# Expert rows put into block order during the mixer, and experts from the third on loading plain blocks, in a one-layer hybrid encoder step

## The chip, the cores and the metric

The kernel runs on one core of one Trainium2 chip. The metric is device time in microseconds (us) of one execution, the median of several. Times inside an execution are microseconds from the first instruction of the profile.

## The reference

One encoder layer runs over 1,104 tokens of width 1024: 64 sample tokens with a carried state, and a prompt of 16 meta and 1024 ordinary tokens. Everything is float32.

```python
xn = rmsnorm(x, norm_mix)
mix = token_mixer(xn, ...)        # trailing pooling + gated linear attention, then w_out
h = x + mix
hn = rmsnorm(h, norm_ffn)
# hier_moe: one expert group of 4, then the top 2 of its 8 experts, with gates
g = argmax(softmax(hn @ w_rg + b_rg)); top_i = top_k(le of group g, 2)
for each expert e of 32:          # D = 1024, hidden width 512
    y = (silu(xb @ w_eg[e]) * (xb @ w_eu[e])) @ w_ed[e]     # xb: the rows routed to e
h = h + sum of the two experts' rows, each times its gate
y = rmsnorm(h, norm_final)
```

Each expert takes about 69 rows on average (two picks of 1,104 tokens over 32 experts).

## The kernel before

Tokens lie in 9 tiles of 128 rows (48 rows of the first are padding). The kernel has two long stages, a passage between them and an end.

**The mixer** (`body(i)` on every engine, 0 to about 475 us) handles a tile in 51.5 us. TensorE (PE) projects, VectorE (DVE) does gates, recurrences and routing, ScalarE (ACT) the activations, GpSimd (POOL) the window sums (`windows`, L472 to L483). The tail of tile j runs inside the body of later tiles: ACT's `back_h(j)` writes the normalised rows into the tile `hs` (L642) and stores them twice (once for each pick) into the DRAM tensor `hn_rows` (L646); `back_route` finds the experts; in `body(j + 2)` DVE's `back_rank(j)` gives each row its rank in its expert's list, PE's `mark` turns ranks into a table `idx_f` (row numbers of each of 96 slots of each of 32 experts), and `back_idx` adds it up.

**The passage** (about 475 to 492 us). The last tile is finished piecewise: `own_added`, `own_turned` and `router_own` for its router, `back_route` (L946 to L973), then `ranks(8)` on PE (L1443), `last_rank` on DVE (L1005 to L1015), `mark(8)` on PE (L1449), and `idx_i` (L1097) with the final indices. POOL waits for `idx_i` and gathers the rows of expert 0 and 1 by indirect DMA (L502), PE turns expert 0's rows (`turn_rows`, L1260), DVE scales them (`rows_turned`, L1113), and the first `up` starts (L1564). PE runs idle matmuls in the gaps (`keep_busy`).

**The experts** (about 492 to 1033 us). For each of 32 experts PE does the gate product (128 matmuls), the up product (128), the turning of the next expert's rows, and the down product. Buffers alternate by `b`. The hidden values come over ACT and DVE: ACT takes exp of the gate product (L735), DVE forms the silu (L1120 to L1122) and multiplies the two halves of the up product (L1126), which `down` waits for (`hid_ready`). POOL gathers the rows of an expert when a buffer is free, and scatters an expert's results to `pick_rows` (L513). SP, whose program is in order, issues the three weight loads of each expert (2 MB each): gate (L410) when the gate product two experts back is done, up (L416) when its up product is done, down (L419) when its down product is done. The passage's own order on SP is: gate, up and down of expert 0 and gate of expert 1 from 440.7 us; then it waits for `pe_half_out` and expert 0's rows before up and down of expert 1.

**The end** (about 1033 to 1082 us): each tile's two result rows are loaded, combined, normalised and stored.

Buffers are shared between the stages: `ye[0]`, into which ACT writes the results of even experts, is the tile `kz_v`; `ye[1]` is `hs`; `rows[0]` is `window_work`; `rows[1]` is `xs`.

Of the kernel before, what the change touches and what calls it, by code (L numbers as in the profile page):

```python
# [28 lines left out]
P = 128  # L29
# [35 lines left out]
PICK_ROWS = PICKS * TILES * P  # L65
OUT_ROWS = [SAMPLE] + [P] * (TILES - 1)
# [6 lines left out]
START_BUSY, ROUTE_BUSY, GATHER_BUSY = 54, 24, 34  # L73
# [12 lines left out]
           ("valid", 1), ("block_edge", EXTRA_PER_E), ("iota_x", EXTRA), ("edge_x", EXTRA)]  # L86
# [8 lines left out]
def constants():  # L95
# [16 lines left out]
    put("pick", p + TILES * P * np.arange(PICKS)[None, :] - NO_ROW)  # L112
    put("valid", (p < SAMPLE) | (p >= SAMPLE + PADS))
    put("block_edge", BLOCK * (1 + np.arange(EXTRA_PER_E))[None, :])
# [43 lines left out]
def build(nc, x_all, state_pool, state_gla, norm_mix, w_in, w_gate_up, b_gate, w_pool, pool_scale, gla_norm, w_out,  # L158
          norm_ffn, w_router, b_router, w_eg, w_eu, w_ed, norm_final, const,
          y_prompt, y_sample, pool_prompt, gla_prompt, pool_sample, gla_sample):  # L160
    hn_dram = nc.dram_tensor("hn_rows", (PICK_ROWS, D), F32, kind="Internal").ap()
    y_dram = nc.dram_tensor("pick_rows", (PICK_ROWS, D), F32, kind="Internal").ap()

    with ExitStack() as ctx:
# [131 lines left out]
        rowsT = [xnT[:, :, 0:BLOCK], hnT[:, :, 0:BLOCK]]  # L296
        sig = mixT[:, 0:3, :].rearrange("p k n -> p (k n)")
# [5 lines left out]
        rows_idx = [sb(f"rows_idx{b}", [BLOCK, 1], I32) for b in range(2)]  # L303
# [8 lines left out]
        def lot(n):  # L312
# [9 lines left out]
            pe_router pe_rank pe_idx pe_half_out pe_own_T pe_first_rows pe_hist_T pe_small_T  # L322
# [6 lines left out]
            pe_eT pe_g pe_u2 pe_d sig_ready hid_ready eT_ready ye_ready row_idx_ready  # L329
# [9 lines left out]
        out_ready = [sem(f"out_ready{i}") for i in range(TILES)]  # L339
# [14 lines left out]
        def _(sp):  # L354
# [46 lines left out]

            sp.wait_ge(s["s_sample_ready"], 1)
# [5 lines left out]
            def load_weights(t, b):  # L408
                e = 2 * t + b
                sp.dma_start(wg[b], w_eg[bass.ds(e * D, D), :].rearrange("(p k) n -> p k n", k=KD)).then_inc(g_in[b], 16)  # L410
                if isinstance(t, int) and b == 1:
                    sp.wait_ge(s["pe_half_out"], 2)
                    sp.wait_ge(rows_in[0], 16)
                if not isinstance(t, int):
                    sp.wait_ge(s["pe_u2"], 2 * (e - 1))
                sp.dma_start(wu[b], w_eu[bass.ds(e * D, D), :].rearrange("(p k) n -> p k n", k=KD)).then_inc(u_in[b], 16)  # L416
                if not isinstance(t, int):
                    sp.wait_ge(s["pe_d"], e - 1)
                sp.dma_start(wd[b], w_ed[bass.ds(e * FF, FF), :].rearrange("(k p) n -> p k n", p=P)).then_inc(d_in[b], 16)  # L419

            sp.wait_ge(s["pe_v"], TILES)
            load_weights(0, 0)
            load_weights(0, 1)
# [6 lines left out]
            with sp.Fori(1, NE // 2) as t:  # L430
                for b in range(2):

                    sp.wait_ge(s["pe_g"], 2 * t + b - 1)
                    load_weights(t, b)
# [17 lines left out]
            for i in range(TILES):  # L452
                for k, y in ((0, y1[i]), (1, y2[i])):
                    at_row = (k * TILES + i) * P
                    sp.dma_start(y[0:OUT_ROWS[i], :], y_dram[at_row:at_row + OUT_ROWS[i], :]).then_inc(y_in[i], 16)
            for i in range(TILES):
                sp.wait_ge(out_ready[i], 1)
# [8 lines left out]
        def _(pool):  # L466
# [17 lines left out]

            pool.wait_ge(s["history_in"], 1)
            windows(0)
            with pool.Fori(1, TILES) as i:
                windows(i)

            pool.wait_ge(s["idx_ready"], 1)
            pool.wait_ge(s["hn_stored"], 16 * PICKS * TILES)

            def gather(t, b):
                e = 2 * t + b
                if isinstance(t, int):
                    index = idx_i[:, e:e + 1]
                else:
                    index = rows_idx[b][:, :]
                    nc.gpsimd.tensor_copy(index, idx_i[:, bass.ds(e, 1)]).then_inc(s["row_idx_ready"], 1)  # L500
                    wait_parted(pool, s["row_idx_ready"], e - 3, s["parted"])
# [1188 lines left out]
```

## Time and profile before

| what | value |
|---|---|
| median of 3 runs | 1086.74 us (1085.78 to 1088.23) |
| the profiled execution's own time | 1084.18 us |
| its span, first to last instruction | 1082.3 us |
| PE busy | 1015.9 us, 94% |
| DVE, ACT, POOL busy | 418.9, 241.0, 108.5 us |
| chain that ended last | PE 91%, DVE 4%, DMA 2% |
| mean granted PE clock | 0.974 |
| DMA moved | 262.34 MB |

The chain of work that ended last is the span followed back from the last instruction. It is PE's nearly everywhere: so what matters is where PE stands still, and which clock it is granted. The share of DMA time is small in the mixer and near full in the experts.

### The profile page before, as it was taken

How to read it: one execution, taken by the hardware profiler on the slowest of the kernel's cores; microseconds unless marked ns; L12 is line 12 of the kernel's file. 1: busy time of each engine (PE TensorE's matmuls, PEld its weight loads, DVE VectorE, ACT ScalarE, POOL GpSimd, SP SyncE). 2: the span in 40 equal slices, each digit the busy share in tenths (PEclk: the TensorE clock that was granted, in tenths of full speed). 3: DMA queues.
4: the chain of work that ended last, by engine and by line, in shares of the span. 5: the costliest groups of instructions: out<-in, count | busy, mean ns of one | idle time of the engine just before them, and what ended most of it. 6: DMA issues, size and time to landing. Idle time of an engine off the chain costs nothing.

```text
span 1082.3 us, 33080 instructions
## 1 busy us (share of the span) xinstructions
PE 1015.9 (94%) x14746; PEld 827.0 (76%) x14746; DVE 418.9 (39%) x910; ACT 241.0 (22%) x509; POOL 108.5 (10%) x168
## 2 busy tenths in 40 slices
PE   8999999999999999989999999999999999999910
PEld 8786777768685959457888988889888898888810
DVE  2334443535262535362623323233232332323338
ACT  2442232323332322130110111111111111111123
POOL 0110101010100101001010111101111011110000
PEclk9999999999999999999999999999999999999965
DMA  9900010000000000629999999999999999999667
GB/s 331 347 19 40 1 40 0 39 0 39 0 39 20 18 39 1 274 115 332 402 404 398 406 405 399 412 401 406 404 395 408 392 406 394 387 402 384 272 226 297
DMA packets 53075, 262.34 MB, mean 242 GB/s; under 512 B 10301, under 2 KB 12925, under 8 KB 44842
## 3 DMA queue, kind: packets, MB, share of 16 engines
q1 hardware_dynamic: 43274, 234.20, 54.9%
q0 software_dynamic: 7168, 18.10, 5.0%
q10 hardware_dynamic: 2592, 9.44, 2.1%
q8 instruction: 32, 0.52, 0.2%
q14 instruction: 9, 0.07, 0.0%
HBM read 242.00 MB, written 26.80 MB: 248 GB/s over the span
## 4 chain that ended last, share of the span: by engine, by line
PE 91%; DVE 4%; DMA 2%; issue 1%; ACT 1%; SPq 0%; ACTq 0%; POOLq 0%; DVEq 0%
PE bank L1564 32%; PE bank L1279 18%; PE bank L1400 11%; PE bank L1575 10%; PE bank L1331 6%; PE bank L1581 6%; PE bank L1260 4%; DVE arena L1238 1%; PE bank L1380 1%; DVE arena L1236 1%; DVE arena L1244 1%; DMA arena<-in_w_in 1%; PE bank L1338 1%; PE bank L1397 1%; DMA arena<-pick_rows 1%
## 5 line engine op out<-in xcount | busy, mean ns | idle before, releaser
L1279 PE MATMUL bank<-xnT,arena 128*128 128x128 f32 x1728 | 201.0, 277 | 3.1 <-DMA arena<-in_w_in 1.8
L1279 PEld LDWEIGHTS bank<-xnT,arena 128*128 128x128 f32 x1728 | 196.8, 193 | 5.5 <-DVE sA L862 3.5
L1564 PEld LDWEIGHTS bank<-xnT,arena 128*64 128x64 f32 x4096 | 170.4, 137 | 6.5 <-issue 6.2
L1564 PEld LDWEIGHTS bank<-hnT,arena 128*64 128x64 f32 x4096 | 169.6, 137 | 7.5 <-issue 7.5
L1564 PE MATMUL bank<-hnT,arena 128*64 128x96 f32 x4096 | 173.0, 246 | 0.5 <-issue 0.5
L1564 PE MATMUL bank<-xnT,arena 128*64 128x96 f32 x4096 | 173.4, 247 | 0.0
L1120 DVE TENSOR_SCALAR mixT<-mixT 128x384 f32<-128x384 f32 x32 | 11.8, 368 | 319.5 <-ACT mixT L735 319.5
L1400 PE MATMUL bank<-arena,mixT 128*128 128x512 f32 x256 | 111.7, 593 | 0.0
L1400 PEld LDWEIGHTS bank<-arena,mixT 128*128 128x128 f32 x256 | 47.9, 190 | 57.2 <-issue 57.1
L1575 PE MATMUL bank<-arena,silu_r 128*32 128x384 f32 x768 | 85.8, 487 | 0.5 <-issue 0.5
L1581 PE MATMUL bank<-arena,osq 128*32 128x256 f32 x384 | 86.0, 380 | 0.0
L1581 PE MATMUL bank<-arena,silu_r 128*32 128x256 f32 x384 | 85.9, 380 | 0.0
L1575 PE MATMUL bank<-arena,osq 128*32 128x384 f32 x768 | 85.8, 488 | 0.0
L1121 DVE RECIPROCAL mixT<-mixT 128x384 f32<-128x384 f32 x32 | 81.7, 2552 | 1.1
L1331 PE MATMUL bank<-arena,xnT 128*128 128x512 f32 x144 | 64.8, 592 | 0.0
L740 ACT ACTIVATE kz_v<-bank 96x384 f32<-96x384 f32 x32 | 13.8, 482 | 174.7 <-PE bank L1581 174.7
L740 ACT ACTIVATE hs<-bank 96x384 f32<-96x384 f32 x32 | 13.9, 483 | 174.2 <-PE bank L1581 174.2
L1581 PEld LDWEIGHTS bank<-arena,osq 128*32 128x32 f32 x384 | 40.8, 110 | 15.4 <-issue 0.4
L1581 PEld LDWEIGHTS bank<-arena,silu_r 128*32 128x32 f32 x384 | 40.8, 110 | 15.0
L477 POOL TENSOR_TENSOR window_work<-window_work 128x568 f32<-128x568 f32 x9 | 10.2, 1134 | 397.6 <-ACT window_work L608 397.6
L1331 PEld LDWEIGHTS bank<-arena,xnT 128*128 128x128 f32 x144 | 26.0, 190 | 25.8 <-issue 25.8
L735 ACT ACTIVATE mixT<-bank 128x384 f32<-128x384 f32 x32 | 15.7, 492 | 121.0 <-PE bank L1564 121.0
(228 smaller groups left out, 975.1 us busy)
## 6 DMA issues: line engine op xcount, KB each, us to landing
arena<-in_w_eg SPq DMA_DIRECT2D x32, 2048.0 KB, 15.9
arena<-in_w_eu SPq DMA_DIRECT2D x32, 2048.0 KB, 16.3
arena<-in_w_ed SPq DMA_DIRECT2D x32, 2048.0 KB, 16.5
hn_rows<-hs ACTq DMA_DIRECT2D x18, 512.0 KB, 3.3
arena<-pick_rows SPq DMA_DIRECT2D x16, 512.0 KB, 10.8
arena<-in_w_in SPq DMA_DIRECT2D x3, 2048.0 KB, 11.8
arena<-in_w_out SPq DMA_DIRECT2D x1, 4096.0 KB, 13.5
out_y_prompt<-arena SPq DMA_DIRECT2D x8, 512.0 KB
```

Source lines behind the costliest of these rows:

```text
L735: A(sig[:, 0:NH], bank[2 + b][:, 0:NH], ACT.Exp, scale=-1.0).then_inc(s["sig_ready"], 1)
L740: A(ye[b][:, half * OWN:(half + 1) * OWN], bank[6 + half][0:BLOCK, 0:OWN], ACT.Copy).then_inc(s["ye_ready"], 1)
L1120: moe.then(V.tensor_scalar(gs[:, 0:NH], sig[:, 0:NH], 1.0, None, ALU.add))
L1121: moe.then(V.reciprocal(gs[:, 0:NH], gs[:, 0:NH]))
L1236: final.then(V.scalar_tensor_tensor(out=y1[i][0:r, :], in0=y1[i][0:r, :], scalar=gate_all[0:r, i, 0:1], in1=h_all[0:r, i, :], op0=ALU.mult ...
L1260: return nc.tensor.transpose(out, src, ident[0:n, 0:n])
L1279: last = mm(out, w_in_sb[:, k, a:b], xnT[:, k, :], start=k == 0, stop=k == KD - 1)
L1331: last = mm(bank[6][:, :], xnT[:, k, :], w_in_sb[:, k, V0:R0], start=k == 0, stop=k == KD - 1)
L1400: return mm(out[:, :], mix[:, k, :], w_out_sb[:, k, n * 512:(n + 1) * 512], start=k == 0, stop=k == KD - 1)
L1564: last = mm(out[q * SW:(q + 1) * SW, n * BLOCK:(n + 1) * BLOCK], w[:, k, m * P + q * SW:m * P + (q + 1) * SW], rowsT[b][:, k, :], start=k ...
L1575: last = mm(bank[6 + half][g * TG:(g + 1) * TG, 0:OWN], tokens(k, g), wd[b][:, k, half * OWN:(half + 1) * OWN], start=k == 0, stop=k == KF ...
L1581: return mm(bank[n][TGS * TG:P, c:c + REST], tokens(k, g), wd[b][:, k, 2 * OWN:D], start=k == 0 and c == 0, stop=k == KF - 1, skip_group_c ...
```

## The change

During the mixer every tile's normalised rows are also scattered, once for each pick, into a second DRAM tensor `block_rows`, in which each expert owns 96 consecutive rows. For this:

- SP fills `block_rows` with zero rows once (12.6 MB, DRAM to DRAM), after the loads of the start.
- DVE works out each row's slot (`block_slots`, six or seven small operations) at the end of `back_rank`. For the last two tiles it does so after the first expert's rows are prepared.
- POOL's `sort` issues two indirect DMAs of 128 rows a tile, ahead of the window sums of the tile two later; the last two tiles' sorts come after the gathers of experts 0 and 1.
- From expert 2 on SP loads a plain block of 96 rows, between the up and down weights. Its first row load waits for all 18 sorts, with expert 2's weights behind it.
- ACT waits for all 18 sorts before its first expert, since `hs` and `kz_v` are their sources. In the mixer it waits for a tile's sort before it overwrites `hs`.

The rows of experts 0 and 1 are still gathered from `hn_rows`. Expert 0's gather now leaves out the last tile and so can start before that tile is routed; the last tile's rows are added by a product with a selection matrix (`first_sel`) that DVE makes out of `R`. `mark(7)` moves ahead of `router_own(0)`. The wait for `pool_out_ready` moves from ahead of `down` to ahead of the up product. The pick order of `hn_rows` and `pick_rows` becomes tile by tile.

```diff
@@ SP
+            sp.dma_start(block_dram.rearrange("(a b) n -> a b n", b=PADS),
+                         x_all[SAMPLE:SAMPLE + PADS, :].unsqueeze(0).to_broadcast([NE * BLOCK // PADS, PADS, D])).then_inc(s["blocks_zero"], 16)
...
+            sp.wait_ge(s["pe_half_out"], 2)
+            sp.wait_ge(s["hn_stored"], 16 * PICKS * TILES)
+            load_up(1, 1)
+            sp.wait_ge(s["first_rows_in"], 32)
+            load_down(1, 1)
...
+            sp.wait_ge(s["pe_eT"], 1)
+            sp.wait_ge(s["sorted_stored"], 16 * PICKS * TILES)
+            load_rows(2, 0)
+
+            def load_expert(t, b, last=False):
+                e = 2 * t + b
+                sp.wait_ge(s["pe_g"], e - 1)
+                load_gate(e, b)
+                sp.wait_ge(s["pe_u2"], 2 * (e - 1))
+                load_up(e, b)
+                if not last:
+                    sp.wait_ge(s["pe_eT"], e)
+                    load_rows(e + 1, 1 - b)
+                sp.wait_ge(s["pe_d"], e - 1)
+                load_down(e, b)
@@ POOL
+            def sort(j, index, src):
+                wait_parted(pool, s["slot_ready"], j + 1, s["parted"])
+                for k in range(PICKS):
+                    nc.gpsimd.indirect_dma_start(block_dram, bass.IndirectOffsetOnAxis(ap=index[:, k:k + 1], axis=0),
+                                                 src[:, :, :].rearrange("p k n -> p (k n)"), None,
+                                                 bounds_check=NE * BLOCK - 1, oob_is_err=False).then_inc(s["sorted_stored"], 16)
...
+            with pool.Fori(2, TILES) as i:
+                sort(i - 2, slot_i, hs)
                 windows(i)
...
-            gather(0, 0)
-            gather(0, 1)
...
+            pool.wait_ge(s["first_idx_ready"], 1)
+            nc.gpsimd.indirect_dma_start(rows[0], None, hn_dram[0:EARLY_ROWS, :], bass.IndirectOffsetOnAxis(ap=first_idx[:, :], axis=0),
+                                         bounds_check=EARLY_ROWS - 1, oob_is_err=False).then_inc(s["first_rows_in"], 16)
+            pool.wait_ge(s["idx_ready"], 1)
+            pool.wait_ge(s["hn_stored"], 16 * PICKS * TILES)
+            nc.gpsimd.indirect_dma_start(rows[1], None, hn_dram, bass.IndirectOffsetOnAxis(ap=idx_i[:, 1:2], axis=0),
+                                         bounds_check=PICK_ROWS - 1, oob_is_err=False).then_inc(s["first_rows_in"], 16)
+            sort(TILES - 2, slot_i, hs)
+            sort(TILES - 1, slot_last, hs_last)
@@ ACT, ahead of expert(0, 0)
             act.wait_ge(s["hn_stored"], 16 * PICKS * TILES)
+            act.wait_ge(s["sorted_stored"], 16 * PICKS * TILES)
@@ DVE, the passage
             rank.then(V.tensor_tensor(R[:, :], bank[7][:, 64:64 + NE], counts[:, :], ALU.add))
+            V.tensor_scalar(first_sel, con("iota_block"), R[:, 0:1], first_of_tile, ALU.is_equal, ALU.mult).then_inc(s["first_sel_ready"], 1)
...
+            rows_turned(0, 0, [0])
+            last_expert(j)
+            rows_turned(0, 0, [1])
+            dve.wait_ge(s["pe_idx"], TILES)
+            V.tensor_tensor(idx_i[:, :], idx_f[:, :], bank[7][0:BLOCK, 192:192 + NE], ALU.add).then_inc(s["idx_ready"], 1)
+            dve.wait_ge(s["pe_small_T"], 1)
+            for n in range(2):
+                V.tensor_copy(pool_out[n], bank[4 + 2 * n][0:HIST, :]).then_inc(s["pool_out_ready"], 1)
+            dve.wait_ge(s["sorted_stored"], 16 * PICKS * (j - 1))
+            block_slots(e_all[:, j - 1, :], rank_all[:, j - 1, :], slot_i, step=once)
+            block_slots(e_all[:, j, :], rank_all[:, j, :], slot_last, step=once)
+            back_weights(j)
@@ PE, the passage
-            keep_busy(ROUTE_BUSY)
-            pe.wait_ge(s["idx_added"], TILES)
-            ranks(j)
-            mark(j)
-            keep_busy(GATHER_BUSY)
+            keep_busy(ROWS_BUSY)
+            pe.wait_ge(s["first_rows_in"], 16)
+            for half in range(2):
+                for k in range(4):
+                    c = (4 * half + k) * P
+                    mm(first_bank[half][:, k * BLOCK:(k + 1) * BLOCK], rows[0][:, c:c + P], ident[0:BLOCK, 0:BLOCK], start=k == 0, stop=False,
+                       skip_group_check=True)
+                if half == 0:
+                    pe.wait_ge(s["idx_added"], TILES)
+                    ranks(j)
+            pe.wait_ge(s["hs_ready"], TILES)
+            pe.wait_ge(s["first_sel_ready"], 1)
+            for half in range(2):
+                for k in range(4):
+                    last = mm(first_bank[half][:, k * BLOCK:(k + 1) * BLOCK], hs_last[:, 4 * half + k, :], first_sel, start=False, stop=True,
+                              skip_group_check=True)
+                if half == 0:
+                    last.then_inc(s["pe_first_rows"], 1)
+            last.then_inc(s["pe_eT"], 1)
             mark(j)
```

## Rows read from the trace of the kernel before

**Rows 1.** Windows: length, busy time (x instructions) by engine, granted clock, DMA share, GB/s.
```profile
560.00:1030.00 470.00, 469.49 (x9387) 410.85 (x9383) 145.35 (x197) 69.77 (x168) 67.86 (x108) 1.00 0.99 391
```
**Rows 2.** The chain that ended last, in order of time: start, us, what.
```profile
486.23 4.26 DMA window_work<-hn_rows,idx_i
...
492.15 11.68 PE bank L1564 x256
...
504.63 0.35 PE bank L1575
...
1016.30 10.71 PE bank L1564 x256
```
**Rows 3.** Timeline of PE around the first expert: start, us, what.
```profile
490.62 1.51 PE L1260 MATMUL bank<-cst,window_work 96*128 96x96 f32 x8 [2.63 <-DMA window_work<-hn_rows,idx_i]
...
503.75 0.88 PE L1260 MATMUL bank<-cst,xs 96*128 96x96 f32 x8
```
**Rows 4.** Timeline of DVE in the passage and the first expert.
```profile
482.77 0.19 DVE L1007 TENSOR_TENSOR R<-bank,counts 128x32 f32<-128x32 f32 x1
...
483.80 0.27 DVE L1012 TENSOR_SCALAR at_rank<-cst,rk 128x96 f32<-128x96 f32 x1
...
485.10 0.18 DVE L1097 TENSOR_TENSOR idx_i<-idx_f,bank 96x32 int32<-96x32 f32 x1 [0.57 <-PE bank L1449]
...
486.38 0.67 DVE L1101 COPY sc<-bank 15x512 f32<-15x512 f32 x1
491.54 1.20 DVE L1113 TENSOR_TENSOR xnT<-bank,g_ffn 128x384 f32<-128x384 f32 x2 [4.49 <-PE bank L1260]
...
502.75 0.36 DVE L1126 TENSOR_TENSOR osq<-bank,mixT 128x192 f32<-128x192 f32 x1
```
**Rows 5.** Timeline of ACT, the first expert's exp.
```profile
498.65 0.49 ACT L735 ACTIVATE mixT<-bank 128x384 f32<-128x384 f32 x1 [15.64 <-PE bank L1564]
```
**Rows 6.** Timeline of POOL, the first two gathers.
```profile
486.23 1.13 POOL L502 DMA_INDIRECT window_work<-hn_rows,idx_i  x1 [56.67 <-DVE idx_i L1097]
487.66 0.97 POOL L502 DMA_INDIRECT xs<-hn_rows,idx_i  x1 [0.30 <-issue]
```
**Rows 7.** Windows of the passage, columns as in the first group.
```profile
488.00:490.60 2.60, 0.00 (x0) 0.01 (x1) 0.00 (x0) 0.00 (x0) 0.63 (x1) 1.00 0.76 192
...
492.20:494.00 1.80, 1.80 (x24) 1.80 (x26) 0.53 (x1) 0.00 (x0) 0.95 (x1) 0.50 0.78 300
```
**Rows 8.** DMA of the window 505 to 520 us: totals, and issues with us to landing.
```profile
DMA packets 805, 5.73 MB, mean 382 GB/s; under 512 B 106, under 2 KB 155, under 8 KB 555
...
xs<-hn_rows,idx_i POOLq DMA_INDIRECT x1, 11.0
pick_rows<-kz_v,pick_idx POOLq DMA_INDIRECT x1, 7.5
```
**Rows 9.** The chain near the end: the last scatter, nothing else in flight.
```profile
1035.86 3.42 DMA pick_rows<-hs,pick_idx
```
**Rows 10.** DMA queues of the whole span: packets, MB, share of 16 engines.
```profile
q1 hardware_dynamic: 43274, 234.20, 54.9%
q0 software_dynamic: 7168, 18.10, 5.0%
```
**Rows 11.** Line L410, window 950 to 1000 us: the gate weights of experts 29 to 31.
```profile
L410 SPq DMA_DIRECT2D arena<-in_w_eg x3: 332/339/339, 954.6 to 988.3; - x3
...
DMA to landing us min/median/max: 24.6/24.8/26.0
```
**Rows 12.** The third tile's mixer: DVE, POOL and PE timelines, and a window before it.
```profile
60.00:70.00 10.00, 10.00 (x92) 10.00 (x91) 3.10 (x9) 6.76 (x12) 3.12 (x4) 1.00 0.00 2
...
110.82 0.22 DVE L999 TENSOR_TENSOR M_tok<-M,token 128x64 f32<-128x64 f32 x1
...
116.81 0.17 DVE L1019 TENSOR_SCALAR token<-token 128x2 f32<-128x2 f32 x1 [3.08 <-PE bank L1449]
...
117.26 1.13 POOL L477 TENSOR_TENSOR window_work<-window_work 128x568 f32<-128x568 f32 x1 [47.75 <-ACT window_work L608]
...
120.65 0.90 DVE L844 SCALAR_TENSOR_TENSOR pooled<-window_work 128x128 f32<-128x128 f32 x4 [2.24 <-POOL window_work L483]
...
137.57 1.05 PE L1338 MATMUL bank<-pooled,w_pool_sb 128*128 128x128 f32 x8
```

More of the change, by code:

```diff
@@ L71 @@
 BIG = 3.0e38
-START_BUSY, ROUTE_BUSY, GATHER_BUSY = 54, 24, 34
+START_BUSY, ROWS_BUSY = 54, 44
 TG = 32
@@ L302, in build @@
         assert NH <= 3 * P
-        rows_idx = [sb(f"rows_idx{b}", [BLOCK, 1], I32) for b in range(2)]
+        rk_over = sb("rk_over", [P, PICKS])
+        slot_of = sb("slot_of", [P, PICKS])
+        slot_i = sb("slot_i", [P, PICKS], I32)
+        slot_last = sb("slot_last", [P, PICKS], I32)
+        hs_last = kz_v[:, :].rearrange("p (k n) -> p k n", k=KD)
+        first_idx = sb("first_idx", [BLOCK, 1], I32)
+        x_rows_idx = sb("x_rows_idx", [BLOCK, 1], I32)
         pick_idx = [sb(f"pick_idx{b}", [BLOCK, 1], I32) for b in range(2)]
@@ L338, in build @@
         y_in = [sem(f"y_in{i}") for i in range(TILES)]
-        out_ready = [sem(f"out_ready{i}") for i in range(TILES)]
+        out_ready = sem("out_ready")
         w_in_v = w_in.rearrange("(p k) n -> p k n", k=KD)
@@ L429, in _ @@
             sp.dma_start(pool_prompt, pool_out[1]).then_inc(s["outs_stored"], 16)
[L430 to L434, printed above, removed]
+            sp.wait_ge(s["pe_eT"], 1)
[12 more added lines that the diff above has]
+                load_down(e, b)
+            with sp.Fori(1, NE // 2 - 1) as t:
+                load_expert(t, 0)
+                load_expert(t, 1)
+            load_expert(NE // 2 - 1, 0)
+            load_expert(NE // 2 - 1, 1, last=True)
             sp.wait_ge(s["slots_ready"], 1)
@@ L999, in back_rank @@
                 V.tensor_tensor(M_tok[:, :, :], Mk, token[:, :].unsqueeze(2).to_broadcast([P, PICKS, NE]), ALU.mult).then_inc(s["onehot_ready"], 1)
+                if not slots:
+                    return
+                if not first:
+                    dve.wait_ge(s["sorted_stored"], 16 * PICKS * j)
+                block_slots(e_of, rk[:, :], slot_i, con("pad_row") if first else None)
             def last_rank(j):
@@ L1085, in _, with rows_turned @@
             back_weights(j - 1)
-            back_rank(j - 1)
+            back_rank(j - 1, slots=False)
             own_added(1)
+            back_idx(j - 1)
+            dve.wait_ge(s["idx_added"], TILES)
+            V.tensor_copy(first_idx[:, :], idx_f[:, 0:1]).then_inc(s["first_idx_ready"], 1)
             own_turned(1)
-            back_idx(j - 1)
             back.begin(j)
             back_route(j, last=True)
-            rank.begin(j)
+            rank.base, rank.n = rank.base + rank.n, 0
             last_rank(j)
-            dve.wait_ge(s["idx_added"], TILES)
-            dve.wait_ge(s["pe_idx"], TILES)
-            V.tensor_tensor(idx_i[:, :], idx_f[:, :], bank[7][0:BLOCK, 192:192 + NE], ALU.add).then_inc(s["idx_ready"], 1)
-            back_weights(j)
-            dve.wait_ge(s["pe_small_T"], 1)
-            for n in range(2):
-                V.tensor_copy(pool_out[n], bank[4 + 2 * n][0:HIST, :]).then_inc(s["pool_out_ready"], 1)
             moe = Steps(dve, s["dve_moe"])
-            def rows_turned(e, b):
-                for half in range(2):
+            def rows_turned(e, b, halves=range(2)):
+                for half in halves:
                     if isinstance(e, int) and e == 0 and half == 0:
@@ L1547, in turn_rows @@
             def turn_rows(e, b, count):
-                pe.wait_ge(rows_in[b], count)
+                if isinstance(e, int) and e == 1:
+                    pe.wait_ge(s["first_rows_in"], 32)
+                else:
+                    pe.wait_ge(rows_in[b], count)
                 for half in range(2):
@@ L1552, in turn_rows @@
                         last = turn(bank[half][:, k * BLOCK:(k + 1) * BLOCK], rows[b][:, c:c + P], BLOCK)
-                    if isinstance(e, int) and e == 0 and half == 0:
-                        last.then_inc(s["pe_first_rows"], 1)
                 last.then_inc(s["pe_eT"], 1)
```

131 lines of the change are left out of this document (69 added, 62 removed).

## The prediction

> **What bounds the kernel now.** I read the windows first. From 560 to 1030 us PE is busy for 469.49 of 470.00 us at full clock [rows 1]: the experts are bound by PE, and nothing done to their loads can make that stretch shorter; it can only make it longer, if a load comes late. Then the chain that ended last, for the place where PE does not set the time itself. There is one, the passage: the chain goes through the gather of expert 0's rows, 4.26 us from issue to landing, and the gate and up products of expert 0 start at 492.15 [rows 2]. Last the timelines of each engine there. So the change can act in three places: the passage, the mixer (only where it adds work), and the experts (only by lateness).
>
> Everything below is counted on the start of expert 0's `down`, 504.63 before [rows 2]. From there on PE runs through, and a shift of that start is a shift of the end.
>
> **The passage, PE's part.** Before, `R` is made at 482.77 and the last marks are ready 1.30 later at 484.07; `mark`, `idx_i` at 485.10, the gather, eight turns and the scaling follow [rows 2 to 4, 6]. After, the gather of expert 0 needs only `idx_f` of the first eight tiles, some 6 us earlier, so it lands beside the last tile's routing. The new chain: `mark(7)` ahead of `router_own(0)` costs the routing about 0.1 (an estimate, since part of it stands in a gap); one small DVE operation ahead of `R` 0.15, so `R` at 483.02; `first_sel`, of the shape of the marks (0.27 [rows 4]), at about 483.5; then `last_rank` ends at 484.5 and DVE is free to scale the first half, 0.65 (half of the 1.20 plus the start [rows 4]), until 485.2. PE meanwhile does the four products of that half (half of the 0.88 of eight such [rows 3]) and starts `up` near 485.3. It stops again after eight of the 256 matmuls, because `last_expert` (about 0.65) and the second half (0.6) come first on DVE: it goes on at 486.5. With 10.71 for the 256 matmuls at full clock [rows 2], less the 0.33 done, and 0.81 for expert 1's turns, PE stands before `down` at 497.7 where it stood at 504.63: 6.9 us earlier. If that were all, the time would be some 7 us less. A half-clock stretch as before would take up to 1.7 of it.
>
> **The passage, the new wait.** `down` needs `hid_ready`, this needs ACT's exp of the gate product, and ACT, an in-order engine, now waits ahead of it for all 18 sorts. Behind this wait are the exp, DVE's silu and `down` on PE. When do the last sorts land?
>
> - DVE: `idx_i` after the second half is scaled and `mark(8)` is done, at 486.6; the two copies into `pool_out` take 1.27 (485.78 to 487.05 before, the second is in [rows 4]); so 487.9. Two times `block_slots`, each six operations of about 0.2 with a wait behind each (small ones take 0.17 to 0.22 [rows 4, 12]), 1.3: slots of tile 7 at 489.2, of tile 8 at 490.5.
> - POOL: from `idx_i` to the start of a gather took 0.95 (485.28 to 486.23), and two in a row stand 1.43 apart [rows 4, 6]. So the gather of expert 1 at 487.5, the four sorts at 490.1, 491.4, 492.7 and 494.0.
> - Landing. Below: a scatter with nothing else in flight landed 3.42 after its issue [rows 9], which gives 497.4. Above: beside weight loads a scatter took 7.5 and a gather 11.0 [rows 8], so 505. Between them I count bytes. The 64 gathers and scatters of before moved 18.10 MB [rows 10], 0.28 each; a sort moves 128 rows, 0.52, and the four 2.1 MB. SP issues expert 1's down weights (2.1 MB) when the gather of expert 1 has landed, about 492.5, so they flow from 494 beside the sorts. The sorts' data can flow from 491.8; some 0.7 MB is through by 494, and 1.4 MB is left. At half of the 382 GB/s of [rows 8] that is 7.2, with 0.6 for completion 501.8. I take 501.8, the loaded case, since nothing keeps the weights back; both ends stay for the range.
>
> From the exp at 498.65 to the end of the second half of `hid` and PE's start is 4.85, were the up product ready: 498.65 to 502.75, two halves of 0.36 and the hand-over [rows 4, 5]. So `down` starts at 501.8 + 4.85 = 506.7, 2.1 later than before. PE is idle from 497.7 to 506.7: the 6.9 gained are lost to a stall of 9.
>
> **The clock.** Before, PE stood still from 488.0 to 490.6, and then had half clock until 494.0: 0.50 granted in 492.2 to 494.0 [rows 7], that is 1.2 GHz of 2.4. It paid 1.51 for 0.81 of turns and 11.68 for 10.71 [rows 2, 3], 1.7 in all. Its part in expert 0 is already within 504.63. A stall of 9 us must bring the same again, now behind the start of `down`: +1.7, with 0.8 and 2.6 as bounds for where the stretch falls.
>
> The Trainium skill (TensorE: Matmul & The Clock Gate, Part 1) says that the clock is throttled by default and activity releases it; the rows agree.
>
> **The sum**: +2.1 + 1.7 = +3.8 us. Bounds: sorts at 497.4 give -2.3 + 1.4 = -0.9; at 505 they give +5.2 + 2.0 = +7.2.
>
> The Trainium skill (DMA: Bandwidth & Descriptors, Anatomy of one DMA) puts a transfer from GpSimd at about 2.0 us plus its bytes at 436 GB/s, mostly for the receipt of the write; an estimate from it for the last sort is 3.2 us, landing at 497.2, and the sum would be about -1 in place of +3.8. By this rule, the 3.42 of [rows 9] agrees for an idle machine; the 7.5 and 11.0 of [rows 8] do not, and the sort is issued into the busy case.
>
> **Parts that I cost at nothing.** In the mixer `block_slots` adds 1.5 us to DVE per tile behind L999 (110.82). It is covered by the 3.08 that DVE waits for PE at 116.81 [rows 12]; ACT's steps that follow it have the same gap. Without cover it would be 1.5 x 7 = 10. The sorts take POOL 2.6 before 117.26, in 47.75 of idle time [rows 12]. Their 7.3 MB (seven tiles, twice 0.52) flow where DMA is idle (share 0.00 [rows 12]). Waiting for the previous sort before `slot_i` or `hs` is written again costs nothing with tens of us between. The zero fill, 12.6 MB, starts when the loads end, by 60 [rows 12]. Both its sides are in DRAM, which no row shows: at 382 GB/s it takes 33, at half of that 66, so it ends at 93 to 126. POOL's first sort wants it at 112.5, and the window sums queue behind. PE needs them only at 137.57, and POOL and DVE need 5.6 for it (117.26 to 120.65 and four times about 0.3 [rows 12]): it may end at 129 at no cost.
>
> The Trainium skill (DMA: Bandwidth & Descriptors, Latency and other measured facts) gives 207 to 214 GB/s per direction for copies within HBM at good pitches; an estimate from it is 59 us, an end at 119, still in time. No row here shows such a copy.
>
> SP: the weights of expert 2 now wait for the sorts, 501.8 where gate was issued at 498.7. But up and down of expert 1 are by then done, where before they were in the queue ahead, so gate and up of expert 2 land no later than about 515; they are wanted at 528. The tail is the same work.
>
> **The rivals.**
>
> *Same, because the sorts land soon and the gain and stall cancel*: this is the lower bound, -0.9, 1085.8. It holds if the two streams do not slow each other.
>
> *Faster*: ACT's wait costs less than the early gather saves. The point is a landing of the last sort by 495.9 (504.63 - 2.17 - 1.7 - 4.85). For it POOL must issue without the 0.95 of hand-over, at 489.3 to 493.0, and each land in 3: then `down` starts at 500.9, -3.8, with the clock's 1.7 or 0.8 -2.1 to -3.0, so 1084.2. For it speaks that an idle scatter took 3.42; against it the down weights in the same stretch and the larger sorts.
>
> *Late loads at the end of the experts*: the gate weights of expert 31 were issued at 988.3, landed 26.0 later, and were wanted at 1016.30 [rows 2, 11]: 2.0 to spare. A plain block moves 96 rows (0.39 MB) in place of about 0.28. By [rows 10] 18.10 MB took 54.1 us of the 16 engines and 234.20 took 594: 2.99 and 2.54 per MB, so 0.85 becomes 1.00, +0.15 an expert, 4.5 over 30. The experts begin with about 4 us less of backlog; without this, PE would starve by 2.5 on top: 1093. For it speaks that [rows 1] have DMA at 0.99; against it, that the indirect gathers, which slow their neighbours, are gone.
>
> *The fill is slow*: at a quarter of 382 it takes 132 and ends at 192; PE would stand for 60. Price 60, 1147; unlikely.
>
> **How the numbers follow.** The profiled execution took 1084.18 (span 1082.3 and 1.9 around it), 2.56 below the median of the runs. The forecast is the median plus the sum: 1086.74 + 3.8 = 1090.5. A change within 0.2% (2.17 us) can hardly be told from none. Chances: the wait outweighs, 0.60 (most of it above 2.17, some 0.12 below); the same by cancelling, 0.13; faster, 0.12; late loads on top, 0.10; slow fill and the unforeseen, 0.05. So faster 0.12, same 0.24, slower 0.64. The range takes in the lower bound and the upper one with some starving: 1085.3 to 1096.0; given the likeliest case alone, 1087.5 to 1094.
>
> **What would show it.** In the timeline of PE, eight products of `hs_last` near 483.6 to 484.5 and `up` from 485 to 486.5 with one short stop; then a stall of about 9 before L1575's successor for expert 0, put down to DVE; ACT's first exp near 502, released by a DMA into `block_rows`; granted 0.5 for some 3 us behind the stall. Landings of gate weights below 28 to the end, no waits of PE after 530. Wrong would be: an exp right behind the gate product at 492 (then 7 us are gained); a wait of POOL for the fill beyond 129; waits of PE for weights near 1000.

## The result and the profile after

The changed kernel takes 1135.16 us (median of 4 runs, 1133.08 to 1138.38). The kernel before, on the same chip, takes 1086.26 (4 runs, 1084.32 to 1088.23). The ratio is 1.0453 [1.0421, 1.0484]: slower, by 49 us. The forecast was 1090.5 with a range to 1096.0. The profiled execution has a span of 1133.8 against 1082.3 before, 51.5 more.

First the waits of PE over the whole span (releaser, us in total, times, longest):

```profile
PE bank L1668 <- DMA arena<-in_w_ed: 17.4, 18, 1.7
PE bank L1657 <- DMA arena<-in_w_eu: 11.1, 15, 1.7
PE bank L1657 <- DMA arena<-in_w_eg: 10.7, 12, 1.3
PE bank L1668 <- DVE osq L1203: 7.5, 1, 7.5
PE bank L1355 <- DMA arena<-in_w_in: 2.2, 1, 2.2
```

L1657 is `up`, the gate and up products; L1668 is the first matmul line of `down`. PE waits 45 times for expert weights that are not there, never longer than 1.7 us, 39.2 us in all. The stall of 7.5 is the passage's; the 2.2 are the wait for the first weights of the whole kernel.

The windows of the experts answer to [rows 1]:

```profile
560.00:760.00 200.00, 198.76 (x3941) 172.69 (x3939) 60.40 (x83) 29.34 (x71) 13.33 (x24) 1.00 1.02 383
760.00:1000.00 240.00, 210.63 (x4138) 181.95 (x4136) 64.99 (x86) 30.32 (x73) 13.32 (x24) 1.00 1.02 363
560.00:1030.00 470.00, 434.96 (x8542) 375.75 (x8538) 133.31 (x181) 62.16 (x151) 27.76 (x50) 1.00 1.02 372
```

PE is busy for 434.96 of 470 us where it was for 469.49. The last two columns say why: the 16 DMA engines are busy all the time (share 1.02) and move 383, then 363 GB/s. The kernel before, in the same two windows:

```profile
560.00:760.00 200.00, 200.00 (x4009) 175.23 (x4005) 62.60 (x84) 29.90 (x72) 30.25 (x48) 1.00 1.02 403
760.00:1000.00 240.00, 240.00 (x4772) 209.03 (x4765) 73.05 (x98) 35.38 (x86) 35.34 (x56) 1.00 1.02 397
```

At the same share fewer bytes go through. The landings of the down weights after their issue, by window (500 to 560, 600 to 650, 700 to 750, 800 to 850):

```profile
DMA to landing us min/median/max: 10.5/12.1/13.6
...
DMA to landing us min/median/max: 20.5/20.5/20.5
...
DMA to landing us min/median/max: 29.6/29.6/29.6
...
DMA to landing us min/median/max: 33.8/33.8/33.8
```

A backlog grows by some 10 us in every 100 until a load takes about two experts, then PE waits for most of them. The chain that ended last shows the same turning point: up to 714 it runs through PE, and from there through one load after another.

```profile
703.69 10.71 PE bank L1657 x256
714.40 0.81 PE bank L1336 x8
720.72 29.58 DMA arena<-in_w_ed
755.99 31.53 DMA arena<-in_w_ed
793.21 32.89 DMA arena<-in_w_ed
```

The passage, on ACT and in the chain, answers to [rows 2, 5]:

```profile
504.75 0.49 ACT L775 ACTIVATE mixT<-bank 128x384 f32<-128x384 f32 x1 [20.25 <-DMA block_rows<-kz_v,slot_last]
```

```profile
494.85 9.82 DMA block_rows<-kz_v,slot_last
505.67 2.56 DVE mixT L1198
517.55 10.73 PE bank L1657 x256
```

ACT sat for 20.25 us in front of the exp until the last sort, issued at 494.85, had landed 9.82 later. Expert 1's gate product starts at 517.55, where it was 510.06 before. So the 51.5 us of the span part at this point: 7.5 up to the start of expert 1, 44.8 from there to the gate product of expert 31 (517.55 to 1068.59 is 551.0; 510.06 to 1016.30 was 506.2), and the rest of the span is 0.8 shorter. Of the 44.8, 39.2 are waits for weights; another 3.4 is busy time of the gate and up products (338.1 behind 517 against 334.7 behind 510 before), which no single wait explains, and 2 stay unassigned.

PE in the passage, and the windows behind the stall (the last three columns: granted clock, DMA share, GB/s), answer to [rows 3, 7]:

```profile
485.04 2.00 PE L1627 MATMUL bank<-gate_work,kz_v 128*128 128x96 f32 x16
486.87 0.45 PE L1525 MATMUL bank<-M_tok,at_rank 128*96 128x32 f32 x4
487.25 6.18 PE L1657 MATMUL bank<-xnT,arena 128*64 128x96 f32 x135
493.70 0.42 PE L1657 MATMUL bank<-xnT,arena 128*64 128x96 f32 x5 [0.27 <-issue]
...
501.20 0.88 PE L1336 MATMUL bank<-cst,xs 96*128 96x96 f32 x8
509.62 0.86 PE L1668 MATMUL bank<-arena,osq 128*32 128x384 f32 x3 [7.53 <-DVE osq L1203]
```

```profile
500.00:504.00 4.00, 2.08 (x38) 1.78 (x34) 0.00 (x0) 0.00 (x0) 0.00 (x0) 1.00 0.98 382
504.20:507.60 3.40, 0.00 (x0) 0.00 (x0) 2.29 (x2) 0.49 (x1) 0.00 (x0) 0.56 0.93 293
507.60:511.00 3.40, 1.38 (x13) 0.93 (x17) 2.73 (x6) 0.00 (x0) 0.00 (x0) 0.50 0.94 395
511.00:514.40 3.40, 3.40 (x31) 2.13 (x27) 0.00 (x0) 0.00 (x0) 0.00 (x0) 0.50 1.04 434
514.40:518.00 3.60, 3.60 (x53) 2.34 (x47) 0.00 (x0) 0.40 (x2) 0.00 (x0) 0.94 0.96 383
```

The granted clock goes to 0.50, 1.2 GHz of 2.4, after PE stopped at 502, and it is back near 514.6. The first 5 us of expert 0's `down` run at half clock.

### The profile page after: what moved, and what is told of

The parts are those of the page before. It is cut to its first block, busy times and chain, and to the rows that moved or that the text cites. A ratio compares the mean times of both kernels' runs of the same rounds, so it can differ in the third digit from the quotient of the medians.

```text
span 1133.8 us, 33117 instructions
## 1 busy us (share of the span) xinstructions
PE 1025.1 (90%) x14756; PEld 829.8 (73%) x14756; DVE 427.2 (38%) x968; ACT 240.7 (21%) x509; POOL 86.1 (8%) x129
## 4 chain that ended last, share of the span: by engine, by line
PE 64%; DMA 29%; DVE 5%; issue 1%; ACT 1%; SPq 0%; POOL 0%; ACTq 0%; POOLq 0%; DVEq 0%
DMA arena<-in_w_ed 26%; PE bank L1355 17%; PE bank L1657 12%; PE bank L1476 11%; PE bank L1668 7%; PE bank L1407 5%; PE bank L1674 4%; PE bank L1336 2%; DVE arena L1314 1%; PE bank L1456 1%; DMA block_rows<-kz_v,slot_last 1%; DVE arena L1312 1%; DVE arena L1320 1%; DMA arena<-in_w_in 1%; PE bank L1414 1%
## 5 line engine op out<-in xcount | busy, mean ns | idle before, releaser
L1657 PE MATMUL bank<-xnT,arena 128*64 128x96 f32 x4096 | 176.1, 247 | 13.4 <-DMA arena<-in_w_eu 6.2
L1657 PEld LDWEIGHTS bank<-xnT,arena 128*64 128x64 f32 x4096 | 170.4, 137 | 22.8 <-DMA arena<-in_w_eg 8.1
L1657 PE MATMUL bank<-hnT,arena 128*64 128x96 f32 x4096 | 174.3, 247 | 10.4 <-DMA arena<-in_w_eg 5.4
L1657 PEld LDWEIGHTS bank<-hnT,arena 128*64 128x64 f32 x4096 | 169.9, 137 | 18.7 <-issue 12.3
L1668 PE MATMUL bank<-arena,osq 128*32 128x384 f32 x768 | 88.3, 499 | 16.4 <-DMA arena<-in_w_ed 8.9
L1668 PE MATMUL bank<-arena,silu_r 128*32 128x384 f32 x768 | 85.8, 487 | 9.1 <-DMA arena<-in_w_ed 8.5
L1674 PE MATMUL bank<-arena,osq 128*32 128x256 f32 x384 | 88.4, 388 | 0.0
L1674 PEld LDWEIGHTS bank<-arena,osq 128*32 128x32 f32 x384 | 41.8, 112 | 15.7 <-issue 1.0
L1674 PEld LDWEIGHTS bank<-arena,silu_r 128*32 128x32 f32 x384 | 40.9, 110 | 15.9 <-issue 0.4
L1668 PEld LDWEIGHTS bank<-arena,osq 128*32 128x32 f32 x768 | 31.6, 112 | 27.5 <-issue 18.0
L1668 PEld LDWEIGHTS bank<-arena,silu_r 128*32 128x32 f32 x768 | 31.1, 110 | 19.1 <-issue 10.8
```

Source lines behind the costliest of these rows:

```text
L1657: last = mm(out[q * SW:(q + 1) * SW, n * BLOCK:(n + 1) * BLOCK], w[:, k, m * P + q * SW:m * P + (q + 1) * SW], rowsT[b][:, k, :], start=k ...
L1668: last = mm(bank[6 + half][g * TG:(g + 1) * TG, 0:OWN], tokens(k, g), wd[b][:, k, half * OWN:(half + 1) * OWN], start=k == 0, stop=k == KF ...
L1674: return mm(bank[n][TGS * TG:P, c:c + REST], tokens(k, g), wd[b][:, k, 2 * OWN:D], start=k == 0 and c == 0, stop=k == KF - 1, skip_group_c ...
```

## The experiments

Two questions were open. Which property of the plain row loads slows the weights? And what does the passage cost by itself? Each run's ratio is against the kernel before on the same chip.

**1. No row loads.** Experts 2 to 31 work on what lies in their buffers, and PE does not wait for rows (not shown).

```diff
-                sp.dma_start(rows[b], block_dram[bass.ds(e * BLOCK, BLOCK), :]).then_inc(rows_in[b], 16)
```

> The changed kernel without the row loads of experts 2 to 31 (no wait for them either; these experts work on what lies in the row tiles). Everything else, the zero fill, the sorts and the passage, is kept. Theory A (the plain row loads are what starves PE of weights): the 39 us of PE's waits for weights go away, and about 1091 to 1093 is left, the passage's cost. Theory B (the loss comes from the new order of the SP queue, or from expert 2's weights waiting for the sorts): stays near 1135.

Measured: 1091.36 against 1085.44, 1.0050 [1.0038, 1.0061]. No wait of PE for the experts' weights is left, and gate weights near the end land after 9.9 to 11.0 us. The change costs 48.9 us, this kernel 5.9, each against the kernel before on its own chip. So 43 us hang on these 30 loads of 0.39 MB, and the passage alone costs about 5.9.

**2. The same loads from another place**: 96 rows of the down weights in place of `block_rows`.

```diff
-                sp.dma_start(rows[b], block_dram[bass.ds(e * BLOCK, BLOCK), :]).then_inc(rows_in[b], 16)
+                sp.dma_start(rows[b], w_ed[bass.ds(e * FF, BLOCK), :]).then_inc(rows_in[b], 16)
```

> The changed kernel, but each row load reads 96 rows of 4 KB out of the expert's down weights in place of block_rows, so the rows' values are others; same shape, same tile, same place in the queue. If the place in DRAM (a tensor filled and scattered into a moment before) makes the load dear: down to about 1095. If the shape at the SBUF end (96 partitions, six to an engine, out of step with the weights' eight) or the bytes do: stays at 1130 to 1140.

Measured: 1141.66, 1.0511 [1.0469, 1.0553], 42 us of waits for weights; 1.7 above the upper end of what was expected. The loss does not go away when the source is another tensor that no store has touched: it is not `block_rows`.

**3. The same loads, 128 partitions wide**: 128 rows from the block's first, 0.52 MB. The 32 further rows are the next block's and are not used; `block_rows` gets some more rows at its end for the last block (not shown).

```diff
-                sp.dma_start(rows[b], block_dram[bass.ds(e * BLOCK, BLOCK), :]).then_inc(rows_in[b], 16)
+                sp.dma_start(wide_rows[b], block_dram[bass.ds(e * BLOCK, P), :]).then_inc(rows_in[b], 16)
```

> The changed kernel, but each row load moves 128 rows (the expert's 96 and the 32 behind them, which nothing reads) onto 128 partitions: a third more bytes, in the shape of the weight loads. If the 96-partition shape is what is dear: the waits for weights shrink or go, 1092 to 1105. If it is bytes alone (0.13 MB more for 30 experts, 0.3 us each): 1140 to 1146. If the place in DRAM: 1140 or more.

Measured: 1089.14 against 1085.44, 1.0034 [1.0013, 1.0056]. A third more bytes, and a loss of 3.7 us in place of 48.9; that is below even the range expected for this theory. The windows of this kernel:

```profile
560.00:760.00 200.00, 200.00 (x3988) 174.68 (x3986) 60.46 (x84) 29.82 (x72) 13.34 (x24) 1.00 1.01 421
760.00:1000.00 240.00, 240.00 (x4800) 210.18 (x4800) 75.92 (x102) 34.80 (x84) 15.55 (x28) 1.00 1.02 422
```

421 GB/s at the same busy share where 96 partitions gave 383 and 363; near the end gate weights land after 12.8. PE never waits for them here, so 421 is what the kernel asks for and not a limit of the engines. The queue that carries the weights shows the price. From 700 to 960 us SP's queue moved 105.42 MB at 97.4% of the 16 engines, in the change 91.32 MB at 97.9%: 2.40 us of all 16 engines per MB against 2.79. What slows the DMA engines is the number of partitions that a row load fills.

**4. The 96-row loads issued by GpSimd**, on its own queue, in place of SP, at the points where the kernel before issued its gathers.

```diff
...
+            def pool_rows(e, b):
+                pool.dma_start(rows[b], block_dram[bass.ds(e * BLOCK, BLOCK), :]).then_inc(rows_in[b], 16)
```

> The changed kernel, but the plain loads of 96 rows from block_rows are issued by GpSimd on its own queue, at the points where the kernel before issued its gathers. If being in the same queue as the weights (between up and down) is what costs: down to about 1095. If the load itself slows its neighbours whoever issues it: 1115 to 1140.

Measured: 1112.17, 1.0239 [1.0200, 1.0279]; 393 and 379 GB/s, 23 us of waits. Against 48.9 us the loss is 26.7: half of it goes, half stays. The time lies between the two theories' figures, 3 below the second's range. With the queue the moment of issue changed too, so how much each is worth stays open; but the loads slow the weights from another queue as well, and the place in SP's queue is not the whole cause.

**5. 112 partitions.**

```diff
-                sp.dma_start(wide_rows[b], block_dram[bass.ds(e * BLOCK, P), :]).then_inc(rows_in[b], 16)
+                sp.dma_start(wide_rows[b], block_dram[bass.ds(e * BLOCK, 112), :]).then_inc(rows_in[b], 16)
```

> The kernel with 128-row block loads, but with 112 rows on 112 partitions (seven to an engine). If a load is dear because its split over the 16 engines does not fall on the engines' own partitions, as the weights' split does, 112 is as bad as 96 or worse: 1125 to 1150. If it is dear because 96 partitions fill one half of the row tile more than the other (64 and 32), 112 (64 and 48) stands near 128: 1090 to 1105.

Measured: 1136.2 against 1086.16, 1.0465 [1.0426, 1.0504]; 380 and 372 GB/s. More bytes than 96 and, within two runs 9 us apart, the same loss: it does not come down in proportion as the load gets wider; of the widths run it is gone only at 128.

**6. 128 rows in two loads of 64 partitions**, one behind the other: the bytes of experiment 3 exactly, over all 128 partitions.

```diff
+                for half in range(2):
+                    sp.dma_start(wide_rows[b][64 * half:64 * half + 64, :], block_dram[bass.ds(e * BLOCK + 64 * half, 64), :]).then_inc(rows_in[b], 16)
```

> The row load of 128 partitions (0.52 MB, gate weights landing in 11.7 to 12.9 us, 421 GB/s, 1089.1) is cut into two loads of 64 partitions each, one behind the other; the bytes, the rows and the place in the queue stay. If the number of partitions of a load matters because it decides which of the 16 engines carries which partitions (the split theory: only a load of 128 partitions is cut like the weights'), the halves are out of step as the loads of 96 and 112 were: 340 to 390 GB/s, gate weights landing 28 us or more after issue near the end, waits of PE for weights of 30 us or more, 1125 to 1145. If a partial load was slow because its bytes do not divide evenly over the engines or it leaves the upper partitions out (64 rows of 4 KB divide by 16, and the pair covers all 128), it stays at 1087 to 1092 with landings near 12 and no waits for weights.

Measured: 1164.59 against 1086.74, 1.0716 [1.0656, 1.0775], above even the range that the winning theory gave (two runs, 10 us apart). Its windows and waits:

```profile
560.00:760.00 200.00, 187.29 (x3702) 162.38 (x3699) 56.82 (x78) 27.38 (x66) 12.22 (x22) 1.00 1.02 366
760.00:1000.00 240.00, 202.83 (x3888) 174.76 (x3883) 61.22 (x83) 28.45 (x69) 12.21 (x22) 0.99 1.02 344
```

```profile
PE bank L1660 <- DMA arena<-in_w_eg: 29.6, 20, 2.2
PE bank L1671 <- DMA arena<-in_w_ed: 19.9, 21, 2.0
PE bank L1660 <- DMA arena<-in_w_eu: 15.7, 18, 1.2
```

The same 128 rows into the same 128 partitions cost 1089.1 as one load and 1164.6 as two. With it "the upper partitions are left out" and "the bytes don't divide evenly by 16" fall as causes: 64 rows of 4 KB do divide (and so do 96 and 112). What the fast one has alone is that a single load fills all 128 partitions, as the weights' loads do. Two things stay untested: this experiment also doubles the number of loads, and each half fills only half of the partitions at a time. A split into two loads of 128 partitions with half the columns each would tell the number of loads from the width. For 96 and 112 against 128 partitions the number is the same, so there it is not the reason.

**7. The gathers of the kernel before, widened.** The kernel before, in which only the gathers of experts 2 to 31 change: 128 indices, the last 32 out of bounds, into 128 partitions.

```diff
-        rows_idx = [sb(f"rows_idx{b}", [BLOCK, 1], I32) for b in range(2)]
+        rows_idx = [sb(f"rows_idx{b}", [P, 1], I32) for b in range(2)]
...
-                nc.gpsimd.indirect_dma_start(rows[b], None, hn_dram, bass.IndirectOffsetOnAxis(ap=index, axis=0),
+                nc.gpsimd.indirect_dma_start(to, None, hn_dram, bass.IndirectOffsetOnAxis(ap=index, axis=0),
```

> The kernel before, with only the 30 gathers of experts 2 to 31 changed: 128 indices (the last 32 out of bounds, so that they move nothing) into 128 partitions in place of 96. The passage is the kernel before's. If the shape of the gather sets how fast the weights beside it land, the gate weights of 950 to 1000 land well below the 24.6 to 26.0 of before and DMA moves 405 to 420 GB/s near the end, with the time unchanged (within 0.2%, 1084 to 1088), since PE never waited there. Then the gain of the version with the early first gather and wide gathers is all passage plus weights in time. If the landings stay near 25, the shape of an indirect gather does not matter, and that version's gain over its narrow sister came from elsewhere. A drop of the time below 1082 would say that the experts of the kernel before were not bound by PE alone.

Measured: 1085.79 against 1086.74, 0.9988 [0.9977, 0.9998]. The time is the same, as it must be where PE never waited, but the margin is not. The issues of its window 950 to 1000:

```profile
...
arena<-in_w_eg SPq DMA_DIRECT2D x3, 2048.0 KB, 14.6
...
```

Gate weights land after 14.6, before it was 24.8 [rows 11]. So the gathers of before already had the fault of the plain loads, in a milder form, and the 2.0 us to spare were what it left over.

**8. The exp ahead of the wait.** Experiment 3's kernel, and ACT waits for the sorts only behind the first exp.

```diff
-            act.wait_ge(s["sorted_stored"], 16 * PICKS * TILES)
             expert(0, 0, True)
...
                 act.wait_ge(s["pe_d"], e + 1)
+                if first and b == 0:
+                    act.wait_ge(s["sorted_stored"], 16 * PICKS * TILES)
```

> The kernel with 128-row block loads, with ACT's wait for the 18 sorts moved behind the first expert's exp, ahead of its first write of a result tile. If the wait's place is the whole cost of the passage: PE's 10.6 us before the first down go, and with them the half-clock stretch behind it (some 2.4): 1089.1 - 13 = about 1076, and no less than 1075. If something else is then late (up weights of expert 1, expert 2's weights behind the sorts): 1080 to 1086, with a wait of PE before 530 us in the trace.

Measured: 1081.19 against 1086.16, 0.9963 [0.9949, 0.9976]; faster, but the gain is 5 us short of the first expectation; the time is in the range of the second, without the wait of PE for weights that it names. The stall in front of `down` is gone:

```profile
485.53 6.21 PE L1660 MATMUL bank<-xnT,arena 128*64 128x96 f32 x135
492.02 0.45 PE L1660 MATMUL bank<-xnT,arena 128*64 128x96 f32 x5 [0.28 <-issue]
...
494.91 6.13 PE L1660 MATMUL bank<-xnT,arena 128*64 128x96 f32 x106 [0.49 <-issue]
500.97 0.88 PE L1339 MATMUL bank<-cst,xs 96*128 96x96 f32 x8
501.78 0.52 PE L1671 MATMUL bank<-arena,osq 128*32 128x384 f32 x3
```

`down` starts at 501.78, 7.8 before the change's 509.62. What was not foreseen stands in the middle: 1.6 us of small "issue" gaps with short, slow groups of matmuls between them, and then 106 matmuls in 6.13 where 106 at full clock take 4.43 (10.71 for 256). The 1.7 more are the clock's: from 494.9 to 498.3 the granted clock is 0.55, right behind the gaps. From 485.53 to the turns at 500.97 `up` takes 15.4 in place of 10.7, which is the missing 5. Much the same gaps stand in the change's own `up` (the timeline above), with the clock at 1.00 behind them, and hidden there by the stall; experiments 3 and 10 do not have them. What makes the gaps is open. A block of instructions is fetched between 492 and 494, in the middle of them, but experiment 3 has the same fetch in that stretch and no gap.

**9. Only the early gather.** The change without `block_rows`, without sorts and fill: expert 0's early gather and the split of its rows stay, experts 2 to 31 gather 96 rows as before.

```diff
-            sort(TILES - 2, slot_i, hs)
-            sort(TILES - 1, slot_last, hs_last)
+            pool.wait_ge(s["pe_eT"], 1)
+            gather(1, 0)
+            pool.wait_ge(s["pe_eT"], 2)
+            gather(1, 1)
```

> The changed kernel without block_rows: no zero fill, no slots, no sorts, no wait for them; experts from the third on gather their rows on GpSimd as before. The early gather of expert 0 and the passage's new order stay. If the early gather is worth what the prediction put it at (6.9 us) and all the loss comes with the block rows: 1085.4 - 6.9 = 1078.5, up to 1080 with the clock. If the early passage itself costs something: 1083 or more.

Measured: 1085.46 against 1086.16, 1.0001 [0.9985, 1.0016]. Expert 1's gate product starts at 505.61, 4.4 earlier than before, and the gain is not in the time. PE's waits in the experts show where most of it went:

```profile
PE bank L1642 <- DMA arena<-in_w_eg: 1.7, 4, 0.7
PE bank L1653 <- DMA arena<-in_w_ed: 1.3, 4, 0.4
```

An expert that starts 5 us earlier has 5 us less of loaded weights in hand, and with 96-row gathers the 2.0 to spare did not suffice. From there to the gate product of expert 31 this kernel takes 510.5 (505.68 to 1016.17) where the kernel before took 506.2: there 4.3 are lost. The waits make 3.0 of it; the other 1.3, and the 0.6 by which the end is longer, I cannot place.

**10. The early gather with wide gathers.** Experiment 9 with the 128 indices of experiment 7.

```diff
-                nc.gpsimd.indirect_dma_start(rows[b], None, hn_dram, bass.IndirectOffsetOnAxis(ap=index, axis=0),
+                nc.gpsimd.indirect_dma_start(wide_rows[b], None, hn_dram, bass.IndirectOffsetOnAxis(ap=rows_idx[b][:, :], axis=0),
```

> The same, with every gather of experts 2 to 31 told 128 indices onto 128 partitions, the last 32 of them out of bounds, so that nothing more is moved. The time should equal the run with 96 (PE is the bound in both). If the 96-partition shape is also what slows the gathers' neighbours: the gate weights of experts 29 to 31 land in 12 to 18 us in place of about 25. If the indirect DMA spreads its rows in its own way, whatever the partitions: they land in 22 to 27.

Measured: 1076.90 against 1086.16, 0.9916 [0.9898, 0.9933]. It beats both kernels, and the expectation, by which it should have equalled experiment 9, missed. Its PE has no wait for the experts' weights and no stall; the whole passage:

```profile
484.60 1.11 PE L1603 MATMUL bank<-cst,window_work 96*128 96x96 f32 x8
485.56 2.00 PE L1612 MATMUL bank<-gate_work,kz_v 128*128 128x96 f32 x16
487.39 0.45 PE L1510 MATMUL bank<-M_tok,at_rank 128*96 128x32 f32 x4
487.77 10.78 PE L1642 MATMUL bank<-xnT,arena 128*64 128x96 f32 x256
498.48 0.88 PE L1321 MATMUL bank<-cst,xs 96*128 96x96 f32 x8
499.29 0.52 PE L1653 MATMUL bank<-arena,osq 128*32 128x384 f32 x3
```

`down` starts at 499.29, 5.3 before the kernel before's 504.63, and there is no half-clock stretch: turns take 0.88 for eight and `up` 10.78 for 256. From expert 1 to expert 31 it takes 505.2 us (504.68 to 1009.83), against 510.5 in experiment 9: the start comes early and is not lost again. In the profiled executions that makes 5.4 up to expert 1 and 1.1 after it, less 0.2 at the end, 6.2 in the spans; the medians differ by 9.3, and I cannot place the rest. Experiment 7 gives 0.1% alone, experiment 9 nothing, both together 0.8%: here each is worth something only with the other.

## Why the prediction was wrong

**Failed: the price of a plain row load.** The step is in the rival of late loads: "By [rows 10] 18.10 MB took 54.1 us of the 16 engines and 234.20 took 594: 2.99 and 2.54 per MB, so 0.85 becomes 1.00, +0.15 an expert, 4.5 over 30." That weights would come late was the right kind of loss; its price, 2.5 us, was far too low, and it had a chance of only 0.10. A load was priced by its own bytes at 2.54 per MB, and the weights beside it at nothing more. Experiment 1 against the change gives 48.9 - 5.9 = 43 us for 30 loads, 1.4 us each; experiment 3 shows that the same rows and more cost 3.7 in all, passage included, when they fill 128 partitions. The charge is on all that the 16 engines carry meanwhile: 2.79 us per MB of SP's queue in the change (700 to 960 us), where the sum took 2.54 and experiment 3 has 2.40. An estimate from the first two is 0.25 x 6.7 MB = 1.7 us an expert, near the 1.4 measured. "Against it, that the indirect gathers, which slow their neighbours, are gone" was half right: they did slow them (experiment 7: 24.8 to 14.6), but for their width, which the plain loads kept.

**Failed with it: "Landings of gate weights below 28 to the end, no waits of PE after 530".** The down weights took 29.6 by 700 and 33.8 by 800. A margin of 2.0 us over 30 experts was read as safe because the loads' shape was taken for granted.

**Right in mechanism, short in size: the passage.** The early gather did free the gate and up products, and ACT's wait for the 18 sorts did give it back; the exp was released by a DMA into `block_rows`.
- `up` started at 487.25, without the stop after eight matmuls that was foreseen (485.3, and on at 486.5). `R` came at 484.33, 1.3 later than the 483.02 counted: 0.8 was lost by the mixer's end, 0.4 of that in a wait for its own first weights (2.2 against 1.8), and 0.5 in the routing, beyond what had been put for it.
- The last sort landed at 504.67, foreseen 501.8 with 505 as the loaded end. It was issued 0.85 late (494.85) and took 9.82, where 7.8 was counted, 0.6 of them for a completion that no row or run shows by itself. The idle 3.42 [rows 9], and with it the lower bound, was far off.
- From there to `down` took 4.95 (4.85 foreseen), so `down` started 5.0 late, not 2.1.
- The clock cost 2.5 (7.49 - 4.99), foreseen 1.7 with 2.6 as bound: the half-clock stretch behind the restart was 5 us in place of 3. Its length does not follow the stall's: experiment 4 stood still for 7.66 us and had half clock for about 2.6 behind it, experiment 2 for 12.10 and about 4.1.
- The sum is +7.5 in this execution, foreseen +3.8, bound +7.2. Medians without late weights say +3.7 (experiment 3) and +5.9 (experiment 1), both inside the range: with the passage alone it would have held. That +3.7 comes so near the +3.8 forecast is luck, since the terms above were short and these two kernels differ by 2.2.

**Right: the parts at nothing.** `block_slots`, the sorts in the mixer and the fill show no cost on PE: the last ranks of the mixer start at 474.16, and in experiment 10, which has none of the three, at 474.64. The slack for the window sums had a slip in it (117.26 to 120.65 and 0.90 for the four are 4.3, not 5.6) that changes nothing. POOL's first sort went at 113.84 and its next window sum at 117.71, released by ACT, not by the fill:

```profile
113.84 1.10 POOL L528 DMA_INDIRECT block_rows<-hs,slot_i  x1 [43.90 <-issue]
...
117.71 1.13 POOL L516 TENSOR_TENSOR window_work<-window_work 128x568 f32<-128x568 f32 x1 [1.34 <-ACT window_work L647]
```

**Right: what bounds the kernel.** "It can only make it longer, if a load comes late" is what happened. Experiment 7 confirms PE as the bound from the other side: loads that land 10 us sooner leave the time alone.

## What to carry to other kernels

A transfer that shares the DMA engines with a stream of 128-partition loads is best tried with 128 partitions in one load, be it plain or a gather, even at the price of rows that are not used: here 96, 112 and twice 64 all slowed the stream. Its cost is to be looked for in what its neighbours take per MB and in when they land, and not in its own bytes. GB/s alone misleads: where PE never waits, it is only what the kernel asks for. Where PE is the bound and DMA stands at a share of 1.0, the landing time of the loads, followed over the whole loop, is the margin, and each change that starts the loop earlier or slows the loads spends it. An in-order engine that must wait for stores should do so behind the operation that PE needs next, not in front of it.

## What the runs showed of the hardware that was not expected

- Row loads beside 2 MB weight loads of 128 partitions, DMA share 1.00 to 1.02, 760 to 1000 us, with PE waiting for weights: one of 112 partitions 372 GB/s, one of 96 363, two of 64 344. With PE never waiting, so that the figure is what the kernel asks for: no row load 391, one of 128 partitions 422 (31 more, which is the 0.52 MB of each expert over 16.9 us), gathers of 96 indices 397, of 128 (32 of them void) 406.
- A DMA share near 1.0 does not tell whether there is slack: it is 1.00 where gate weights land after 10.6 us (experiment 1) and 1.02 in the change, where they come late.
- The same 96-row load from GpSimd in place of SP: 379 GB/s, 23 us of waits in place of 39.
- The last scatter of 128 rows (0.52 MB), issued beside weight loads and behind three others, landed 9.82 us later; with nothing else in flight 96 rows had taken 3.42 [rows 9].
- In the change and in experiments 5, 8 and 9 PE has small gaps put down to "issue" in the first `up` (1.6 us in experiment 8, with 3.4 us at a granted clock of 0.55 behind them; one gap of 0.25 in experiment 9), in the other kernels none. Their cause is open.
